# A two-layer encoder step on one Trainium2 core: another opening, and the first norm of a layer begun in the layer before

## The reference

```
h = RMSNorm(x);  proj = h @ w_in            # pool, window q/k/v, latent q, latent kv, rotary key, gates
A = pooled means of 2/4/8/16 frames, minus the frame, mapped and scaled
B = window attention (QK-norm, sinks, T5 relative-position bias from rel_bias)
C = latent attention: c_kv = rmsnorm(kv_lat); keys and values = c_kv @ w_kvup; QK-norm; softmax over the past
x = x + (sum_i sigmoid(gate_i) * (branch_i @ w_branch_i)) @ w_out
x = x + (silu(g) * u) @ w_down,  [g, u] = RMSNorm(x) @ w_gate_up
```

## Time and profile before

| | us |
|---|---|
| median of 3 runs | 1129.44 |
| lowest, highest | 1125.9, 1129.67 |
| the profiled execution's own time | 1130.26 |
| its span, first to last instruction | 1128.4 |
| PE busy in it | 1081.7 (96%) |
| DVE, ACT, POOL busy | 653.5, 503.6, 293.5 |
| mean granted clock of TensorE | 0.983 |

### The profile page before, as it was taken

How to read it: one execution, slowest core, us unless ns; L and a number is a source line. 1 busy time by engine, 2 the same in 40 slices (tenths; PEclk the granted TensorE clock), 3 DMA queues, 4 the chain that set the end, 5 groups by cost and what they waited for, 6 DMA issues and landing times.

```text
span 1128.4 us, 21279 instructions
## 1 busy us (share of the span) xinstructions
PE 1081.7 (96%) x7524; PEld 1041.3 (92%) x7524; DVE 653.5 (58%) x1042; ACT 503.6 (45%) x862; POOL 293.5 (26%) x220
## 2 busy tenths in 40 slices
PE   5798899999999999999989989999999999999998
PEld 4687899889999999999977979989999999999998
DVE  5658765344575655554367678554446766666443
ACT  4453645444454444432254436545444544444322
POOL 2434334562121111100024424455421211111000
PEclk9899999999999999999989989999999999999999
DMA  6514423323443444444423243232243444444443
GB/s 201 199 39 121 135 76 112 113 95 113 164 155 119 164 149 150 149 163 149 151 95 117 75 126 130 76 113 94 94 150 138 143 158 159 149 149 149 153 149 119
DMA packets 46822, 148.04 MB, mean 131 GB/s; under 512 B 8184, under 2 KB 11352, under 8 KB 46744
## 3 DMA queue, kind: packets, MB, share of 16 engines
q1 hardware_dynamic: 40472, 144.07, 37.2%
q10 hardware_dynamic: 6272, 2.92, 1.0%
HBM read 143.75 MB, written 3.22 MB: 130 GB/s over the span
## 4 chain that ended last, share of the span: by engine, by line
PE 82%; DVE 6%; issue 4%; DMA 2%; ACT 2%; POOL 2%; SPq 0%; ACTq 0%; DVEq 0%; POOLq 0%
PE psum L423 24%; PE psum L425 24%; PE psum L424 24%; DVE Q L1445 1%; DMA scratch<-brel 1%; POOL wsum L1582 1%; PE psum L526 1%; PE psum L553 1%; PE psum L546 1%; ACT WH L813 1%; PE psum L558 1%; DVE stdk L1165 1%; DVE tR L1443 1%; PE psum L599 1%; PE psum L578 0%
## 5 line engine op out<-in xcount | busy, mean ns | idle before, releaser
L423 PE MATMUL psum<-AH,WH 128*128 128x320 f32 x1344 | 427.8, 318 | 15.5 <-DVE AL L1153 13.3
L424 PE MATMUL psum<-AL,WH 128*128 128x320 f32 x1344 | 420.4, 313 | 0.0
L425 PE MATMUL psum<-AH,WL 128*128 128x320 f32 x1344 | 420.3, 313 | 0.0
L423 PEld LDWEIGHTS psum<-AH,WH 128*128 128x128 f32 x1344 | 257.2, 191 | 27.1 <-DVE AL L1153 16.5
L424 PEld LDWEIGHTS psum<-AL,WH 128*128 128x128 f32 x1344 | 257.4, 191 | 1.1 <-issue 0.6
L425 PEld LDWEIGHTS psum<-AH,WL 128*128 128x128 f32 x1344 | 257.0, 191 | 0.0
L813 ACT CAST WH<-raw 128x1024 fp32r<-128x1024 f32 x178 | 185.3, 1045 | 159.2 <-PE psum L425 149.6
L1542 POOL TENSOR_TENSOR WL<-raw,WH 128x1024 fp32r<-128x1024 f32 x66 | 163.3, 2486 | 223.2 <-ACT WH L813 223.2
L1139 DVE TENSOR_TENSOR WL<-raw,WH 128x1024 fp32r<-128x1024 f32 x110 | 134.8, 1227 | 142.7 <-ACT WH L813 135.7
L1313 DVE TENSOR_TENSOR WL<-raw,WH 128x1024 fp32r<-128x1024 f32 x88 | 107.5, 1222 | 49.4 <-ACT WH L950 48.2
L950 ACT CAST WH<-raw 128x1024 fp32r<-128x1024 f32 x86 | 88.5, 1040 | 48.9 <-PE psum L425 48.9
(11 more groups left out here) (227 smaller groups left out, 1575.2 us busy)
## 6 DMA issues: line engine op xcount, KB each, us to landing
raw<-w_all SPq DMA_DIRECT2D x267, 512.0 KB, 3.2
X<-x_in SPq DMA_DIRECT2D x2, 640.0 KB, 5.2
y_out<-X SPq DMA_DIRECT2D x2, 640.0 KB, 4.0
ckv<-lat_in ACTq DMA_DIRECT2D x2, 512.0 KB, 5.2
lat_out<-ckv ACTq DMA_DIRECT2D x2, 320.0 KB, 3.0
scratch<-brel SPq DMA_DIRECT2D x1, 510.0 KB
cst<-cst_in SPq DMA_DIRECT2D x1, 481.0 KB, 9.0
bias<-scratch SPq DMA_DIRECT2D x8, 48.0 KB, 2.6
```

Of the source, the lines that this page charges most:

```text
L423: mm(out, WH[:, slot, c0:c0 + cols], high, start=first, stop=False)
L424: mm(out, WH[:, slot, c0:c0 + cols], low, start=False, stop=False)
L425: return mm(out, WL[:, slot, c0:c0 + cols], high, start=False, stop=last)
```

## The change

- The opening. SP issues unit 0 first, then par, the two small table inputs, units 1 to 3, the constants. ACT issues X in three parts (chunks 0-1, 2-3, 4-7). DVE zeroes `ssum`, PE makes five products on these zeros (`WARM`), then the table product. The self-copy of X is gone; `x_ready` is counted by clearing a spare block of `par`.
- The table. `brel` has a place of its own. The first five rounds of the ring (`EARLY` = 6) are written out on SP, so that units 4 and up are loaded as soon as slots are free; the table is written in eight parts, one behind each of units 8 to 15, and read in eight, one behind each of units 16 to 23.
- The norms. Chunks 0 to 3 of a layer's first norm are handled ahead of the layer loop for the first layer, and inside the second half of the down projection for the next one. They are also made behind the last layer, on zero gains, where nothing uses them. The loop body begins with chunks 4 to 7. `two_dense` is cut at chunk 4: both units on 0 to 3, both on 4 to 6, the sum, both on 7. It waits there for the banks 4 and 5 (`summed`).
- ACT's order. The cast of unit 3 goes ahead of the wait for the constants and of five DMA issues; the copy `ckvH` of the cached latents goes behind the square of `kvr` and the cast of unit 6.
- The end. X is written out in eight parts instead of two.

```diff
     def _(sp):
-        sp.dma_start(par[:], par_in).then_inc(s.par_in, 16)
-        sp.dma_start(X[:, 0:4, :], x_in[:, 0:4, :]).then_inc(s.x_in0, 16)
         sp.dma_start(raw[:, 0, :], w_all[0]).then_inc(raw_ready[0], 16)
-        sp.dma_start(X[:, 4:8, :], x_in[:, 4:8, :]).then_inc(s.x_in1, 16)
+        sp.dma_start(par[:, 0:DEPTH * NPAR], par_in).then_inc(s.par_in, 16)
+        sp.dma_start(rb[:], rb_in).then_inc(s.rb_in, 16)
+        sp.dma_start(onehot[:], oh_in).then_inc(s.rb_in, 16)
...
-        sp.wait_ge(s.brel_copied, 1)
-        sp.dma_start(scratch..., brel[:, None, 0:255].to_broadcast([8, 64, 255])).then_inc(s.brel_out, 16)
-        sp.wait_ge(s.brel_out, 16)
-        (eight reads into bias)
+        for i in range(1, EARLY):
+            for q in range(RING):
+                sp.wait_ge(s.split_ready, i * RING + (q - RING + 1))
+                sp.dma_start(raw[:, q, :], w_all[i * RING + q]).then_inc(raw_ready[q], 16)
+                n = (i - EARLY + 4) * RING + q
+                if n < 0:
+                    continue
+                if n < 8:
+                    if n == 0:
+                        sp.wait_ge(s.brel_copied, 1)
+                    sp.dma_start(scratch...[n:n + 1, :, 0:255],
+                                 brel[n:n + 1, None, 0:255].to_broadcast([1, 64, 255])).then_inc(s.brel_out, 16)
+                    continue
+                n -= 8
+                if n == 0:
+                    sp.wait_ge(s.brel_out, 128)
+                (read n into bias)
-        for h in range(2):
-            sp.wait_ge(s.x_ready, 16 * DEPTH + 4 * h + 4)
+        for k in range(KC):
+            sp.wait_ge(s.x_ready, 16 * DEPTH + k + 1)
...
     def _(pe):
-            for k0, k1 in ((0, KC - 1), (KC - 1, KC)):
+            for k0, k1 in zip(cuts, cuts[1:]):
...
+                        if summed is not None:
+                            pe.wait_ge(s.x_ready, summed + q + 1)
...
+        pe.wait_ge(s.warm_zero, 1)
+        for _ in range(WARM):
+            mm(psum[:, tbank(3), 0:T], ssum[:, 0:128], ssum[:], start=True, stop=True)
         pe.wait_ge(s.rb_in, 32)
         mm(psum[0:8, 0, 0:256], rb[:], onehot[:], start=True, stop=True).then_inc(s.brel_mm, 1)
-        pe.wait_ge(s.brel_copied, 1)
...
     def _(act):
-            for k in range(4):
+            for k in range(4, KC):
                 norm_chunk(l, 0, k, square=False)
-            for k in range(4):
+            for k in range(4, KC):
                 norm_chunk(l, 0, k, high=False)
-            for k in range(4, KC):
-                norm_chunk(l, 0, k)
+            high(l, 3)
...
-            for u in range(U_DOWN, NU):
-                high(l, u + LEAD)
+            for i in range(FC):
+                high(l, U_DOWN + i + LEAD)
+                if FC // 2 < i <= FC // 2 + 4:
+                    norm_chunk(l + 1, 0, i - FC // 2 - 1)
...
     def _(dve):
+        v.memset(ssum[:], 0.0).then_inc(s.warm_zero, 1)
+        v.memset(par[:, DEPTH * NPAR:(DEPTH + 1) * NPAR], 0.0).then_inc(s.x_ready, KC)
+        first_low(0)
+        dve.wait_ge(s.par_in, 16)
+        for k in range(4):
+            norm_low(0, 0, k)
+        first_low(1)
         dve.wait_ge(s.brel_mm, 1)
         v.tensor_copy(brel[:], psum[0:8, 0, 0:256]).then_inc(s.brel_copied, 1)
...
+        first_low(2)
...
                     low(l, U_DOWN + half * (FC // 2) + i + LEAD)
+                    if half == 1 and 2 <= i < 6:
+                        norm_low(l + 1, 0, i - 2)
...
     def _(pool):
+        pool.wait_ge(s.brel_mm, 1)
+        sum_squares(0, 0, 1, 4)
         with pool.Fori(0, DEPTH) as l:
-            sum_squares(l, 0)
+            sum_squares(l, 0, 4)
...
+            sum_squares(l + 1, 0, 1, 4)
```

More of the change, by code:

```diff
@@ L107, in __init__ @@
     def __init__(self, sem):
-        self.x_in0 = sem("x_in0")
-        self.x_in1 = sem("x_in1")
+        self.x_in = [sem(f"x_in{i}") for i in range(3)]
+        self.warm_zero = sem("warm_zero")
         self.par_in = sem("par_in")
@@ L389, in _ @@
         sp.dma_start(cst[:], cst_in).then_inc(s.cst_in, 16)
[L391 to L397 removed]
+        for i in range(1, EARLY):
[8 more added lines that the diff above has]
+                        sp.wait_ge(s.brel_copied, 1)
+                    sp.dma_start(scratch.rearrange("h (q r) -> h q r", r=257)[n:n + 1, :, 0:255],
+                                 brel[n:n + 1, None, 0:255].to_broadcast([1, 64, 255])).then_inc(s.brel_out, 16)
[3 more added lines that the diff above has]
+                    sp.wait_ge(s.brel_out, 128)
+                hq, t = divmod(n, 4)
+                src = scratch[n, 63:63 + 64 * 256].rearrange("(q r) -> q r", q=64)[:, 0:BAND]
                 sp.dma_start(bias[hq * 64:hq * 64 + 64, t, :], src).then_inc(s.bias_in, 16)
[L399 removed]
+        with sp.Fori(EARLY, DEPTH * NU // RING) as i:
             for q in range(RING):
@@ L441, in dense, with two_dense @@
             last.then_inc(s.tile_full, 1)
-        def two_dense(l, u, banks, ah, al, ready, value, done, between=None):
-            for k0, k1 in ((0, KC - 1), (KC - 1, KC)):
+        def two_dense(l, u, banks, ah, al, ready, value, done, between=None, cuts=(0, KC - 1, KC),
+                      summed=None):
+            for k0, k1 in zip(cuts, cuts[1:]):
                 if k1 == KC and between is not None:
@@ L955, in ffn_pair @@
                     A(fth[:, p, :], fa[:, p, :], ACT.Tanh, scale=0.5).then_inc(s.th_ready, 1)
-        act.dma_start(rb[:], rb_in).then_inc(s.rb_in, 16)
-        act.dma_start(onehot[:], oh_in).then_inc(s.rb_in, 16)
-        for u in range(LEAD):
-            act.wait_ge(raw_ready[u], 16)
-            nc.scalar.copy(WH[:, u, :], raw[:, u, :]).then_inc(s.high_ready, 1)
-        act.wait_ge(s.par_in, 16)
+        act.dma_start(X[:, 0:2, :], x_in[:, 0:2, :]).then_inc(s.x_in[0], 16)
+        act.dma_start(X[:, 2:4, :], x_in[:, 2:4, :]).then_inc(s.x_in[1], 16)
+        act.dma_start(X[:, 4:8, :], x_in[:, 4:8, :]).then_inc(s.x_in[2], 16)
+        act.wait_ge(s.x_in[0], 16)
+        for k in range(2):
+            norm_chunk(0, 0, k, high=False)
+        act.wait_ge(raw_ready[0], 16)
+        nc.scalar.copy(WH[:, 0, :], raw[:, 0, :]).then_inc(s.high_ready, 1)
+        act.wait_ge(s.par_in, 16)
+        for k in range(4):
+            if k == 2:
+                act.wait_ge(s.x_in[1], 16)
+            norm_chunk(0, 0, k, square=False)
+        act.wait_ge(raw_ready[1], 16)
+        nc.scalar.copy(WH[:, 1, :], raw[:, 1, :]).then_inc(s.high_ready, 1)
+        act.wait_ge(s.x_in[2], 16)
+        for k in range(2, 4):
+            norm_chunk(0, 0, k, high=False)
+        act.wait_ge(raw_ready[2], 16)
+        nc.scalar.copy(WH[:, 2, :], raw[:, 2, :]).then_inc(s.high_ready, 1)
         with act.Fori(0, DEPTH) as l:
-            for k in range(4):
+            for k in range(4, KC):
                 norm_chunk(l, 0, k, square=False)
-            for k in range(4):
+            for k in range(4, KC):
                 norm_chunk(l, 0, k, high=False)
-            for k in range(4, KC):
-                norm_chunk(l, 0, k)
+            high(l, 3)
             act.wait_ge(s.cst_in, 16)
@@ L979, in _ @@
             act.dma_start(vT[:, 256:384], lay(swv_in).rearrange("a p n -> (a p) n")).then_inc(s.cache_v, 16)
-            high(l, 3)
             root_stream(l, 0)
@@ L1320, in ffn_pair, with first_low @@
                     ffn_low(l, j, p - 1)
+        def first_low(u):
+            dve.wait_ge(s.high_ready, u + 1)
+            TT(WL[:, u, :], raw[:, u, :], WH[:, u, :].bitcast(F32), ALU.subtract).then_inc(s.split_ready, 1)
+        v.memset(ssum[:], 0.0).then_inc(s.warm_zero, 1)
+        v.memset(par[:, DEPTH * NPAR:(DEPTH + 1) * NPAR], 0.0).then_inc(s.x_ready, KC)
+        first_low(0)
+        dve.wait_ge(s.par_in, 16)
+        for k in range(4):
+            norm_low(0, 0, k)
+        first_low(1)
         dve.wait_ge(s.brel_mm, 1)
         v.tensor_copy(brel[:], psum[0:8, 0, 0:256]).then_inc(s.brel_copied, 1)
-        dve.wait_ge(s.x_in0, 16)
-        for k in range(KC):
-            if k == 4:
-                dve.wait_ge(s.x_in1, 16)
-            v.tensor_copy(X[:, k, :], X[:, k, :]).then_inc(s.x_ready, 1)
-        for u in range(LEAD):
-            dve.wait_ge(s.high_ready, u + 1)
-            TT(WL[:, u, :], raw[:, u, :], WH[:, u, :].bitcast(F32), ALU.subtract).then_inc(s.split_ready, 1)
-        dve.wait_ge(s.par_in, 16)
+        first_low(2)
         with dve.Fori(0, DEPTH) as l:
             step[0] = 0
-            for k in range(KC):
+            for k in range(4, KC):
                 norm_low(l, 0, k)
@@ L1527, in link, with sum_squares @@
             pool.wait_ge(s.pool_step, l * POOL_STEPS + step[0])
-        def sum_squares(l, which):
+        def sum_squares(l, which, k0=1, k1=KC):
             c = 16 * l + 8 * which
-            for k in range(1, KC):
+            for k in range(k0, k1):
                 pool.wait_ge(s.sq_ready, c + k + 1)
```

23 lines of the change are left out of this document (10 added, 13 removed).

## The result

| us | before | after |
|---|---|---|
| median (runs beside each other) | 1128.45 (4) | 1108.74 (4) |
| lowest, highest | 1125.9, 1129.67 | 1107.8, 1109.41 |
| profiled execution | 1130.26 | 1107.8 |
| its span | 1128.4 | 1106.0 |
| mean granted clock | 0.983 | 0.989 |

The ratio is 0.9832, with an interval from 0.9815 to 0.9849. The gain in medians is 19.7 us where 14.6 were forecast; 1108.7 lies just under the range of 1110 to 1122.

What follows compares the result with a forecast made beforehand. PE was busy for 96% of the span, so only its waits and slow clock, mostly in the two layer openings, could be won. 7.0 + 7.2 + 0.4 = 14.6 us gave 1115 us, range 1110 to 1122.

Steps and rivals of the forecast that it cites:

- the first opening: First layer's start up to the first key product: key products at 39.4 instead of 47.04, 7.0 us gained after the crossing.
- upper end: Top of the first opening's range: 9.0 us gained, if the DMA issues are 1.4 us faster.
- the crossing: First layer's chain behind rstd: DVE's adds wait behind POOL's low parts of units 6 and 7; 0.6 us lost, 0 to 2.4.
- Key product = rstd + 16.66: Both layers: the first key product comes 16.66 us after rstd starts, as in the second layer before.
- The second opening: Second layer's start: rstd at 579.6 instead of 586.83, 7.2 us gained, range 3.3 to 7.9.
- The bubble: PE idle behind the loop's branch at the second layer's start, 1.3 us, hidden before and now bare.
- Additions: Extra norm work in each down phase and the table in eight parts: hidden under other work, costing nothing.
- The end: Last writes of X in smaller parts: 0.4 us gained, range 0 to 1.2.
- Less: Rival: crossing costs 2.4 us in the first layer and the clock falls in the second; gain 8.5, time 1121, chance 0.12.
- swallowed: Rival: table parts hold up weights of units 8 to 23; at 4.6 us each, 1125 (no change), chance 0.06.
- slower: Rival: table parts hold up weights of units 8 to 23; at 6 us each, 1137, chance 0.04.
- More: Rival: PE, not ACT, bounds the first opening, key products at 35.5; 1113 with half, 1111 with all, chance 0.08.

Runs made afterwards that it cites:

- the two pairs: Kernels before and after, each profiled once, then each profiled again unaltered: spans 1128.4 and 1106.0 us, then 1127.0 and 1108.06.
- e5_table_only: Kernel before with only the bias table changed: eight parts behind units 8 to 15, reads behind 16 to 23; 1123.91 us.
- e10_three_issues_late: Kernel after with three of ACT's five DMA issues moved behind the cast of unit 7; 1109.26 us.
- e4_act_order: Kernel after with ACT's old order: cast of unit 3 behind the DMA issues, ckvH copy before the square of kvr; 1113.0 us.
- e1_norm_behind: Kernel after with the next layer's norm of chunks 0 to 3 behind the down projection's last units, not between them; 1115.43 us.
- e6_q_on_dve: Kernel after with the queries' low parts (units 22 to 24) moved from POOL to DVE; 1107.97 us.
- e8_unrolled: Kernel after with the layer loop written out twice on PE, ACT, DVE and POOL; 1108.78 us.
- e9_unrolled_q: Kernel after with the layer loop written out and the low parts of units 22 to 24 made by DVE; 1103.95 us.
- e2_table_first: Kernel after with the table written in one DMA and read in eight ahead of unit 4; 1123.97 us.
- e3_no_warm: Kernel after without the five products on zeros; 1112.5 us, six runs in two groups.

## Why the prediction was wrong

- **The failed step: the first opening, 7.0 us.** It gave 10.1 and 11.9 in the two pairs, beyond the upper end of 9.0 as well. Of the 3.1 us missing in the first pair 2.45 are in rstd (22.7 forecast, 20.25 measured), 0.6 is the crossing that didn't come. In rstd the five DMA issues were mis-sized: 4.7 us from 16.2, where it was 3.2 from 14.75. They do not wait for the arithmetic ahead of them, and the length was taken from a row in which the table's write was filling the queues (`e5_table_only` shows 3.25 without it); I had put that 1.4 into the upper end only. With the issues right, my own line for POOL (sum ready at 19.1) and the 1.45 us from POOL's last sum to rstd in the kernel after would have set rstd near 20.6. `e10_three_issues_late` shows it: ACT is not what binds.
- **The crossing, 0.6 taken, 0 to 2.4.** It is real and costs 2.1 (`e4_act_order`), but ACT's new order makes DVE come first; for that I had counted nothing. (The other thing that the order gives, 0.8 us of rstd, the sum had, as the cast of 1.05.) And I took before's 21.10 us for a fixed number, where two other profiles of that order have 23.46 and 23.51. A second crossing belongs as much to the old kernel's price as to the new one's risk; that is 2.4 us on the side of the gain which no bound of mine held.
- **Key product = rstd + 16.66.** Right: 16.67 and 16.66, no wait for the square of kv.
- **The second opening, 7.2.** 6.7 and 5.8. The sum put rstd 11.24 us behind the first add (579.6 - 568.36); it was 11.73, mis-sized by 0.5: DVE started its AL 0.2 later and took 3.66 for them, not 3.4. The other 0.9 of the second pair is before's own stretch, 18.47 and then 17.53. The clock stayed at 1.00. The bubble was 1.76, not 1.3 (1.4 by the rows, 570.7 - 569.30), with a branch 0.36 us longer than in before, but PE then waits for AL and it costs nothing more.
- **Additions, nothing.** The table's parts held no cast of ACT for raw, and the stretch from key product to the window's squares is 59.2 in before's second profile and in after. The set of norms in the down phase cost nothing that the stretches show; bare, behind the last layer, it cost 2.7 (`e1_norm_behind`, 4 forecast). Whether the products on zeros help is open: with them the clock was low at the first products or soon after, in both profiles; without them half of the runs were 5 us longer.
- **The end, 0.4.** 0.6.
- **The total.** The three terms together gave 17.4 and 18.3 where 14.6 were forecast. The medians moved by 19.7 and 19.1. The 0.8 to 2.3 between are in no term: about 1.4 is the loss by crossings estimated at `e6_q_on_dve`, the rest is open.
- **Rivals.** Less, swallowed and slower are out. "More" had the right sign, and its 1111 lies nearest to the time, but for the wrong reason: it took PE's chain to the key product for the bound, at 35.5, where rstd plus 16.66 still holds and rstd is set by POOL's sums and PE's wait for AL. Its chance of 0.08 was too small, since it was the same error in the same row that the upper end named.

## What to carry to other kernels

When a block goes away, take again the durations that were measured beside it: ACT's issues measured while a large DMA filled the queues were an upper end here, not the middle, and they started before the arithmetic ahead of them was done. Then follow every engine to the join, the point where all must meet, and forecast by the one that is last with these numbers. Two operations of DVE and POOL that start within some tenths of a microsecond of each other make a time that is a draw: profile before twice, and move one of them to the other engine before timing small edits, since `e8_unrolled` and `e9_unrolled_q` show that a sound gain of 2.4 us can otherwise be lost in it.

## What the runs showed of the hardware

- **Who is first.** A 32x320 operation on DVE took 0.48 us alone and 2.46 to 2.59 beside a POOL subtraction of 2.4 to 2.6; the low part of the cached latents (`ckvL`) took 3.32 where POOL was 0.3 ahead, and 1.23 where DVE was 0.4 ahead, POOL's then 3.06. This agrees with the Trainium skill, SBUF — State Buffer, "SBUF: two separate sides" (an exclusive lock for whichever starts first). What I had not expected is that it makes up much of the scatter of the kernel: 10 us over 29 runs of before, 3 us over 12 beside them with three subtractions moved; and 3.6 us over 5 runs of the unrolled kernel, 0.9 over 5 with them moved. The scatter differs by group as well (before's 9 runs beside these last two lay within 3.7), so only kernels of one group can be compared in it.
- **An issue can be held.** ACT's issue of krT, a 64 KB load, took 0.47 us without the table's write, 1.78 and 1.29 in the two profiles of before, and 4.13 in `e2_table_first`, where the write began 1.5 us ahead of it.
- **The loop's turn.** The branch between the layers lasted 3.7 us in before and 4.07 in after on PE's queue; it runs ahead of the products, so only 1.76 us were bare on PE, but DVE stood for 3.54. Without it the second opening was 2.4 us shorter (`e8_unrolled`).
- **The clock's record.** It can read 1.00 at the start of an execution while the products are spaced 0.27 us, as at its low level: from 9.2 to 12.8 us in `e3_no_warm`, from 13.7 to 16.6 in the kernel before.
